# Expert rows added by TensorE in the second half of a gather, four routes moved to the first half, and copies moved to ScalarE

## The chip, the cores and the metric

The kernel runs on one core of a Trainium2 chip. The metric is the device time of one execution in microseconds. The core's engines work side by side and each takes its instructions in the order of its program: TensorE (matmuls, in the profile PE), VectorE (DVE), ScalarE (ACT), GpSimd (POOL) and SyncE (SP, which issues loads and stores). They wait for one another by semaphores. Matmul results go to eight PSUM banks of 128 x 512 float32.

## What is computed

512 tokens of width 1024 pass two blocks. The first block is a convolution mixer and then a layer of experts: each token has 8 heads, each head picks 16 of 16384 experts, and each expert is a row of u (1024 numbers) and a row of v (1024 numbers):

```
idx, gates = peer_route(q, sub_keys)          # 8 heads x 16 experts for every token
act = gelu(einsum("chkd,cd->chk", u[idx], xc))
out = einsum("chk,chkd->cd", act * gates, v[idx])
```

The second block is a feed-forward layer (hidden 2816), two causal attentions side by side (a forget-gate one, and a latent one with rotary parts), a gated mix, an output product and another feed-forward layer, over the 512 tokens.

## The kernel before, in words

Tokens stand on the 128 partitions in four tiles (t = 0 to 3). The expert layer is a loop over 512 "rows". Row i is head and choice (16 rows to a head, 8 heads to a tile): one indirect DMA by GpSimd gathers, for the 128 tokens of the tile, u and v of one chosen expert each (1 MB) into one of 7 `pair` buffers. Groups of 16 rows are one route (head n of 32). For every row:

- `dot(i)` on VectorE (the custom instruction of line 1321) multiplies u with the token and sums;
- `weigh(i)` on ScalarE makes the weight in five small activations (all activations have line 1384);
- in the first half (rows 0 to 255, tiles 0 and 1) ScalarE makes a diagonal of the weights (`diag`), and TensorE adds weight times v into a pair of banks ("mix") by two matmuls of 512 columns, which the profile shows as four records; in the second half (rows 256 to 511, tiles 2 and 3) VectorE adds it to `resid` itself, two rows later (`add_row`, line 827);
- then the buffer is free and GpSimd issues the gather of row i+7 into it (line 1862).

`route(n)` on VectorE finds the 16 best experts of head n in 24 small steps. It runs during the 16 rows before, four steps a row for six rows; GpSimd can't gather row 16n before. Index and gate buffers are four deep.

Chain A is the whole second block for tiles 0 and 1 (256 tokens). It runs in the second half of the gather, chain B (tiles 2 and 3) behind the gather. Each engine has the chain's steps in the same order. `plan_banks()` writes by hand which PSUM bank each step uses and when it is due on a plan clock in us: feed-forward 1 from 0 to 244, norm before the projections from 252, projections to 327, the 32 looks (a look is query times key for one head and one tile of queries) from 330.2 to 429.4 every 3.2 us, gates, branches and output to 558, feed-forward 2 to 802. `clock(row)` turns a row's number into this clock, 3.3 us a row from row 268 on. VectorE, ScalarE and GpSimd go through rows and, behind each row, do all chain steps due by its clock (`Paced.until`). TensorE has no rows in the second half and goes through chain A as fast as data come.

A look's path in attention: TensorE look n, VectorE its row's least (line 1144), ScalarE the exponential, TensorE turns the result of look n-3, VectorE copies the turned one (line 1151), TensorE multiplies with the values (n-4). During the first 16 looks `prepared` also makes the latent heads out of two banks, four steps a look, on all engines.

Weights come in 1 MB chunks through three buffers, issued by SyncE, a chunk when the one three before it has been used.

The lines that matter:

```
                for k in range(16):
                    i = 16 * n + k
                    dot(i)
                    if i >= HALF + 2:
                        add_row(i - 2)
                    for _ in range(4):
                        next(steps, None)
                    ...
                    first.until(clock(i))
```

Of the kernel before, what the change touches and what calls it, by code (L numbers as in the profile page):

```python
# [7 lines left out]
P = 128  # L8
# [77 lines left out]
ROW_US = 3.3  # L86
START_ROW = 268
# [11 lines left out]
class Plan:  # L99
# [14 lines left out]
    def ring(self, stage, n, us=0.0):  # L114
        self.add(stage, [(self.at + j) % 8 for j in range(n)], us)
        self.at = (self.at + n) % 8
# [6 lines left out]
def plan_banks():  # L123
    p = Plan()
    for stage, n in (("norm0", 10), ("cf", 16), ("sc", 16), ("bg", 4), ("ms_sc", 1), ("mean", 1), ("wout0", 4),
                     ("var", 1), ("ms_cf", 1), ("wout1", 4)):
        p.ring(stage, n)
    p.add("hn", [0, 1])
    for c, (h, a, b) in enumerate(CALLS):
        p.add("q", [0, 1])  # L130
        p.add("S", [2, 3])
        if c == 0:
            p.add("hn", [0, 1, 2, 3, 0, 1])
    for t in range(2):
        p.add("mix", [4, 5] if t % 2 == 0 else [6, 7], told=False)
    p.clock = 0.0
    for x in "AB":
        p.at = 0

        def ffn(f):  # L140
            p.clock += 8.0
            p.ring(f"norm{f}{x}", 4, 1.5)
            p.ring(f"up{f}{x}", 22, 7.0)
            p.ring(f"down{f}{x}", 4, 19.0)

        ffn(1)
        p.clock += 8.0
        for stage, n, us in (("norm_m", 4, 1.5), ("lat", 2, 5.0), ("fq", 2, 7.0), ("fv", 2, 7.0), ("cum", 1, 3.0),
                             ("tfq", 4, 1.0), ("fk", 2, 7.0), ("tfk", 4, 2.0), ("tlat", 2, 1.0)):
            p.ring(stage + x, n, us)  # L150
        p.add("look" + x, [0, 1] * 16, 3.2)
        p.add("turn" + x, [2, 3] * 16)
        p.add("prep" + x, [6, 7] * 8)
        for blk in range(4):
            p.add("o" + x, [4 + blk % 2], told=False)
            p.add("fin" + x, [4 + blk % 2], 4.0)
        p.at = 0
        for stage, n, us in (("gate", 8, 7.0), ("br", 16, 1.8), ("wo", 4, 7.0)):
            p.ring(stage + x, n, us)
        ffn(2)  # L160
    return p
# [62 lines left out]


def clock(row):

    return (row - START_ROW) * ROW_US


def program(nc, x, meta, wts, uv, rows, cols, pos, ident, tri, mask, out):
    with ExitStack() as ctx:
# [98 lines left out]
        MISC, CHAIN, PAIR = 2048, 3216, RAW - 2048 * NPAIR  # L331
# [19 lines left out]
        gat = ar("gat", MISC + 992, 64).rearrange("p (b n) -> p b n", b=4)  # L351
        idx = ar("idx", MISC + 1056, 64, U).rearrange("p (b n) -> p b n", b=4)
        sm = ar("sm", MISC + 1120, 16).rearrange("p (b n) -> p b n", b=4)
# [13 lines left out]
        fsq = ar("fsq", LAYER + 9728, 1024)  # L367
        fsg = [ar(f"fsg{i}", LAYER + 10752 + 256 * i, 256) for i in range(2)]
# [5 lines left out]
        YM = [ar(f"ym{i}", LAYER + 8704 + 512 * i, 512) for i in range(2)]  # L374
        PTB = {"A": [ar(f"pta{i}", LAYER + 9728 + 256 * i, 256) for i in range(4)],
# [48 lines left out]
        def taken(e, stage, n):  # L424

            b = B[stage, n]
            e.wait_ge(outs[b.bank], b.after)

# [45 lines left out]
        def products(e):  # L474
# [122 lines left out]
            scores(2)  # L597
            for i in range(HALF):
                t, r = divmod(i, 128)
                if i % 16 == 0 and i // 16 < 6:  # L600
                    scores(i // 16 + 3)
                e.wait_ge(diagd, i + 1)
                for h in range(2):
                    if r == 0:
                        fresh("mix", 2 * t + h)
                    b = B["mix", 2 * t + h]
                    ins = mm(bank[b.bank][:], diag[i % 8], pair[i % NPAIR][:, 1024 + h * 512:1536 + h * 512], r == 0,
                             r == 127)
                ins.then_inc(v_used, 1)
# [8 lines left out]
            def rows_times(stage, n0, pieces, lhs, ready=None, width=512):  # L618
# [3 lines left out]
                for key, nk in pieces:  # L622
                    w = piece(key, nk)
# [15 lines left out]
            def normed(k):  # L639
                for i in range(2):  # L640
                    turned_rows(k, "norm" + k if k[0] != "m" else "norm_" + k, i, frow[i])
# [5 lines left out]
            def ffn(f, p):  # L647
                normed(f"{f}{p}")
                turned_in(f"norm{f}{p}")
                for c in range(22):  # L650
                    w = piece((f"f{f}", c, p), 8)
# [6 lines left out]
                for h in range(2):  # L658
                    rows_times(f"down{f}{p}", 2 * h, [((f"d{f}", h * 6 + q, p), 4 if q < 5 else 2) for q in range(6)], H,
                               None if h else lambda kt: taken(e, f"up{f}{p}", kt))  # L660
# [8 lines left out]
            def chain(p):  # L669
                t0, nth = T0[p], NTH[p]  # L670
                ffn(1, p)
                normed("m" + p)
                turned_in("norm_m" + p)
                rows_times("lat" + p, 0, [(("lat", 0, p), 4), (("lat", 1, p), 4)], FT, width=360)
                rows_times("fq" + p, 0, [(("fqkv", 0, p), 4), (("fqkv", 1, p), 4)], FT)
                rows_times("fv" + p, 0, [(("fqkv", 4, p), 4), (("fqkv", 5, p), 4)], FT)
# [6 lines left out]
                ins.then_inc(done, 1)  # L683
                e.wait_ge(ext_q, 4 * (nth + 1))
                for i in range(2):
                    heads_turned("tfq" + p, 2 * i, 66, FQ[:, i])
                rows_times("fk" + p, 0, [(("fqkv", 2, p), 4), (("fqkv", 3, p), 4)], FT)
                e.wait_ge(ext_k, 4 * (nth + 1))
                for i in range(2):
                    heads_turned("tfk" + p, 2 * i, 66, FQ[:, i])  # L690
                e.wait_ge(lat_scaled, 2 * (nth + 1))
                for i in range(2):
                    o, done = fresh("tlat" + p, i)
# [3 lines left out]
                attention(p)  # L697
                for c in range(8):
                    w = piece(("gate", c, p), 8)
# [6 lines left out]
                for c in range(4):  # L706
                    yt = YFT if c % 2 else YMT
                    if c == 0:
                        for blk in range(4):
                            taken(e, "fin" + p, blk)  # L710
                    w = piece(("br", c, p), 4)
                    for j in range(4):
                        o, done = fresh("br" + p, 4 * c + j)
# [3 lines left out]
                for h in range(2):  # L717
                    rows_times("wo" + p, 2 * h, [(("wo", 2 * h, p), 4), (("wo", 2 * h + 1, p), 4)], MT,
                               None if h else lambda kt: e.wait_ge(m_add, 8 * nth + kt + 1))
                ffn(2, p)  # L720


# [27 lines left out]
            def attention(p):  # L750
                t0, nth = T0[p], NTH[p]
                prep = prepared(p)
                for i in range(2):
# [5 lines left out]
                for n in range(38):  # L759
                    if n == 16:  # L760
# [47 lines left out]

            chain("A")
            chain("B")  # L810


        def vector(e):
# [319 lines left out]
            def attention(p):  # L1133
                t0, nth = T0[p], NTH[p]
                prep = prepared(p)
                for n in range(38):
# [8 lines left out]
                    if 3 <= n < 35:  # L1145
# [114 lines left out]
            def used(i):  # L1260

                if i <= HALF:
                    e.wait_ge(v_used, i)
                else:
                    e.wait_ge(added, i - HALF)

            def route(n):

                t_, h, r = n // 8, n % 8, n % 4
# [15 lines left out]
                if n >= 4:  # L1285
                    used(16 * (n - 3))
# [37 lines left out]
            def add_row(i):  # L1324
# [3 lines left out]
                if i > HALF:  # L1328
                    e.wait_ge(added, i - HALF)
                stt(r, pair[i % NPAIR][:, 1024:2048], wgt[:, i % 8:i % 8 + 1], r, ALU.mult, ALU.add).then_inc(added, 1)  # L1330

            def mixed_in(t):

                e.wait_ge(v_used, 128 * (t + 1))
# [17 lines left out]
            for n in range(32):  # L1352
                steps = route(n + 1) if n < 31 else iter(())
                for k in range(16):
                    i = 16 * n + k
                    dot(i)
                    if i >= HALF + 2:
# [3 lines left out]
                    if n and n % 8 == 0:  # L1361
                        if k == 2 and n <= 16:
                            mixed_in(n // 8 - 1)
                        if k == 6:
                            final_mean(n // 8 - 1)
                        if k == 9:
                            final_row(n // 8 - 1)
                    first.until(clock(i))
                for _ in steps:
                    pass  # L1370
            for i in (PAIRS - 2, PAIRS - 1):
                add_row(i)
            first.until(1e9)
            final_mean(NT - 1)
# [5 lines left out]
        def scalar(e):  # L1380
# [127 lines left out]
            def normed(k, p, ready):  # L1508
                stage = "norm" + k if k[0] != "m" else "norm_" + k
                t0 = T0[p]  # L1510
                for i in range(2):
                    yield when(stage, 0) - 9.0
                    ready(i)
                    squared(k, i, resid[:, t0 + i, :], fsq)
# [66 lines left out]
            def attention(p):  # L1581
                t0, nth = T0[p], NTH[p]
                prep = prepared(p)
                for n in range(38):
# [4 lines left out]
                    if n < 32:  # L1589
# [5 lines left out]
                        if h == 0 and n >= 16:  # L1595
# [3 lines left out]
                            accum_out=ls[a][:, h:h + 1]).then_inc(out_, 1)  # L1599
                    if n < 16:  # L1600
# [108 lines left out]
            def gates(n):  # L1709
                r = n % 4  # L1710
# [3 lines left out]
            def final_row(t):  # L1714
                if t < 2:
                    for h in range(2):
                        taken(e, "mix", 2 * t + h)
                else:
                    e.wait_ge(added, 128 * (t - 1))
                act(HN[t], resid[:, t, :], ACT.Square, accum_out=nss[:, FINAL + t:FINAL + t + 1]).then_inc(fin_sq, 1)  # L1720

            def weigh(i):
# [9 lines left out]
                act(h_, a, ACT.Copy, scale=gat[:, n % 4, k:k + 1]).then_inc(curved, 1)  # L1732
# [9 lines left out]
            for n in range(32):  # L1742
                if n < 6:
                    scores(n + 3)
                for k in range(16):
                    i, j = 16 * n + k, (16 * n + k) % 8
                    weigh(i)
                    if i < HALF:
                        if i >= 8:
                            e.wait_ge(v_used, i - 7)  # L1750
                        e.wait_ge(weighed, i + 1)
                        act(diag[j], idt[:], ACT.Copy, scale=wgt[:, j:j + 1]).then_inc(diagd, 1)
                    if k == 4 and n < 31:
                        gates(n + 1)
                    if k == 3 and n and n % 8 == 0:
# [8 lines left out]
        def pool(e):  # L1764
# [88 lines left out]
            for i in range(PAIRS):  # L1853
# [4 lines left out]
                if NPAIR <= i < HALF + NPAIR:  # L1858
                    e.wait_ge(v_used, i - NPAIR + 1)
                elif i >= HALF + NPAIR:  # L1860
                    e.wait_ge(added, i - NPAIR + 1 - HALF)
                e.indirect_dma_start(pair[i % NPAIR], None, uv, bass.IndirectOffsetOnAxis(  # L1862
                    ap=idx[:, n % 4, k:k + 1], axis=0)).then_inc(pairs_in[i % NPAIR], 16)
                if i > 128 and i % 128 == 12:
# [132 lines left out]
```

## Time and profile before

| | |
|---|---|
| median of 3 runs | 2866.18 us (2854.21 to 2866.60) |
| profiled execution | 2865.02 us |
| its span, first to last instruction | 2863.2 us |
| granted TensorE clock, mean (1 is 2.4 GHz) | 0.906 |
| TensorE matmuls busy | 2312.3 us (81%) |
| VectorE busy | 1629.2 us (57%) |
| ScalarE busy | 1009.8 us (35%) |
| DMA | 758.73 MB, mean 265 GB/s |

Busy time is summed over an engine's instructions; it says nothing about who waits. By VectorE's dots row 0 stands at 336 us, row 256 at 1067, row 344 at 1397, row 368 at 1501, row 398 at 1655 and row 511 at 2078.

### The profile page before, as it was taken

How to read it: one execution, taken by the hardware profiler on the slowest of the kernel's cores; microseconds unless marked ns; L12 is line 12 of the kernel's file. 1: busy time of each engine (PE TensorE's matmuls, PEld its weight loads, DVE VectorE, ACT ScalarE, POOL GpSimd, SP SyncE). 2: the span in 40 equal slices, each digit the busy share in tenths (PEclk: the TensorE clock that was granted, in tenths of full speed). 3: DMA queues.
4: the chain of work that ended last, by engine and by line, in shares of the span. 5: the costliest groups of instructions: out<-in, count | busy, mean ns of one | idle time of the engine just before them, and what ended most of it. 6: DMA issues, size and time to landing. Idle time of an engine off the chain costs nothing.

```text
span 2863.2 us, 25889 instructions
## 1 busy us (share of the span) xinstructions
PE 2312.3 (81%) x8344; PEld 1502.4 (52%) x8344; DVE 1629.2 (57%) x3312; ACT 1009.8 (35%) x3503; POOL 814.2 (28%) x623
## 2 busy tenths in 40 slices
PE   6756888887877773999354598699689997999999
PEld 6744533332222222884222376587278644786884
DVE  3994445546777769877887989887620013501000
ACT  4222255456666664433443443443310012310000
POOL 3651134345555553323342332322200001000000
PEclk9878999999999996999675589899889997799999
DMA  4210478879999998999874789999924431033443
GB/s 157 74 44 15 162 292 361 345 301 421 421 421 421 421 418 315 408 421 420 340 300 147 279 342 421 371 419 420 415 108 148 153 138 41 30 118 135 159 147 132
DMA packets 107159, 758.73 MB, mean 265 GB/s; under 512 B 12032, under 2 KB 12800, under 8 KB 16400
## 3 DMA queue, kind: packets, MB, share of 16 engines
q0 software_dynamic: 73728, 536.90, 46.5%
q1 hardware_dynamic: 33296, 220.18, 20.1%
q8 instruction: 66, 1.08, 0.1%
q14 instruction: 69, 0.57, 0.1%
HBM read 754.94 MB, written 2.10 MB: 264 GB/s over the span
## 4 chain that ended last, share of the span: by engine, by line
PE 42%; DVE 27%; DMA 18%; issue 6%; ACT 5%; POOL 1%; DVEq 0%; SPq 0%; ACTq 0%; POOLq 0%
PE bank L476 41%; DMA pair<-in_uv,idx 18%; DVE resid L827 6%; DVE pair L1321 6%; DVE acc L827 4%; ACT smalls L1384 1%; ACT diag L1384 1%; DVE qm L821 1%; DVE ohb L821 1%; POOL smalls L1825 1%; DVE idu L1248 1%; PE bank L666 0%; DVE scores L1251 0%; DVE idu L1257 0%; PE bank L496 0%
## 5 line engine op out<-in xcount | busy, mean ns | idle before, releaser
L1862 POOL DMA_INDIRECT pair<-in_uv,idx x512 | 636.7, 1244 | 994.9 <-DVE resid L827 586.3
L1384 ACT ACTIVATE smalls<-smalls 128x1 f32<-128x1 f32 x2056 | 540.8, 287 | 727.6 <-DVE smalls L1321 705.9
L1321 DVE CUSTOM_DVE_ANT_0 pair<-pair,hn 128x1024 f32<-128x1024 f32 x512 | 623.8, 1220 | 286.2 <-DMA pair<-in_uv,idx 281.6
L476 PE MATMUL bank<-ft,raw 128*128 128x256 f32 x3328 | 727.1, 382 | 15.2 <-DVE ft L821 15.2
L476 PEld LDWEIGHTS bank<-ft,raw 128*128 128x128 f32 x3328 | 637.3, 192 | 104.1 <-issue 16.3
L476 PE MATMUL bank<-pair,diag 128*128 128x512 f32 x1024 | 500.0, 622 | 126.9 <-ACT diag L1384 126.9
L476 PEld LDWEIGHTS bank<-pair,diag 128*128 128x128 f32 x1024 | 180.6, 192 | 442.5 <-ACT diag L1384 299.8
L827 DVE SCALAR_TENSOR_TENSOR resid<-pair,smalls,resid 128x1024 f32<-128x1024 f32 x256 | 327.5, 1279 | 0.2
L476 PE MATMUL bank<-raw,hidden 128*128 128x512 f32 x704 | 302.8, 592 | 0.0
L476 PEld LDWEIGHTS bank<-raw,hidden 128*128 128x128 f32 x704 | 133.8, 190 | 166.7 <-issue 166.5
L821 DVE TENSOR_TENSOR hidden<-fsg,bank 128x256 f32<-128x256 f32 x88 | 36.9, 420 | 318.5 <-ACT fsg L1384 317.3
L476 PE MATMUL bank<-xt,half 128*128 128x264 f32 (+1 forms) x864 | 126.1, 311 | 23.5 <-DVE zpad L821 21.0
L1777 POOL TENSOR_TENSOR smalls<-smalls,mh 128x1 f32<-128x1 f32 (+1 forms) x21 | 16.6, 794 | 449.3 <-DVE smalls L824 449.3
L1384 ACT ACTIVATE smalls<-smalls,gat 128x1 f32<-128x1 f32 x512 | 143.0, 279 | 0.0
L496 PE MATMUL bank<-idt,frow 128*128 128x128 f32 x96 | 21.6, 417 | 149.2 <-ACT frow L1384 149.2
L1384 ACT ACTIVATE fsg<-bank 128x256 f32<-128x256 f32 x88 | 33.1, 377 | 307.0 <-PE bank L476 307.0
L476 PEld LDWEIGHTS bank<-xt,half 128*128 128x128 f32 x864 | 120.2, 202 | 29.4 <-DVE zpad L821 17.8
L827 DVE SCALAR_TENSOR_TENSOR acc<-upad,colt,acc 128x512 f32<-128x512 f32 x90 | 123.0, 1367 | 3.0
L476 PE MATMUL bank<-ht,raw 128*128 128x512 f32 (+2 forms) x288 | 114.4, 559 | 1.4 <-ACT ht L1384 1.4
L476 PE MATMUL bank<-raw,ft 128*128 128x512 f32 (+1 forms) x256 | 104.9, 571 | 8.5 <-DVE ft L821 8.5
L1384 ACT ACTIVATE diag<-idt,smalls 128x128 f32<-128x128 f32 x256 | 102.8, 402 | 23.5 <-ACT smalls L1384 0.4
L1771 POOL TENSOR_TENSOR half<-raw,half 128x2048 fp32r<-128x2048 f32 x14 | 66.7, 4770 | 155.2 <-ACT half L1384 155.2
(208 smaller groups left out, 1986.9 us busy)
## 6 DMA issues: line engine op xcount, KB each, us to landing
raw<-in_wts SPq DMA_DIRECT2D x194, 1024.0 KB
pair<-in_uv,idx POOLq DMA_INDIRECT x512
raw<-in_wts SPq DMA_DIRECT2D x10, 512.0 KB
raw<-in_wts SPq DMA_DIRECT2D x4, 720.0 KB
resid<-in_x SPq DMA_DIRECT2D x4, 512.0 KB, 5.4
out<-resid SPq DMA_DIRECT2D x8, 256.0 KB
raw<-in_wts SPq DMA_DIRECT2D x2, 768.0 KB
rowt<-in_rows SPq DMA_DIRECT2D x1, 1204.0 KB, 13.1
```

Source lines behind the costliest of these rows:

```text
L476: return e.matmul(o, a, b, start=start, stop=stop)
L496: ins = e.transpose(o[:, j * P:j * P + n], src[0:n, kt * P:(kt + 1) * P], idt[0:n, 0:n])
L821: return e.tensor_tensor(o, a, b, op)
L827: return e.scalar_tensor_tensor(out=o, in0=a, scalar=s, in1=b, op0=op0, op1=op1)
L1248: e.max_index(di[:, 0:8], dst[:, 0:8], src).then_inc(v_step, vs_.up())
L1321: e.tensor_tensor_reduce(b[:, 0:1024], b[:, 0:1024], HN[i // 128], 1.0, 0.0, ALU.mult, ALU.add, actv[:, i % 8:i % 8 + 1]).then_inc(dotted, 1)
L1384: return e.activation(o, i, f, **kw)
L1771: e.tensor_tensor(half(s)[:, 1, 0:c.n], wbufs[c.slot][:, 0:c.n], half(s)[:, 0, 0:c.n].bitcast(F), ALU.subtract).then_inc(w_lo, 1)
L1777: e.tensor_tensor(nrs[0:n, c:c + 1], nqs[0:n, c:c + 1], mh[0:n, 0:1], ALU.pow).then_inc(n_rs, 1)
L1825: e.tensor_tensor(sm8[(3 * j + 2) % 12][:, 0:k], sm8[(3 * j + 1) % 12][:, 0:k], mh[:, 0:k], ALU.pow).then_inc(hn_rs, 1)
L1862: e.indirect_dma_start(pair[i % NPAIR], None, uv, bass.IndirectOffsetOnAxis(ap=idx[:, n % 4, k:k + 1], axis=0)).then_inc(pairs_in[i % NPAI ...
```

## The change

- `ON_PE` says for every row who adds its v. In the second half it is TensorE for rows 256 to 266 and 338 to 395 (69 rows), VectorE for the rest. `UP_TO[i]` counts how many rows before i each has added, and all waits for "row i is used" go by it.
- TensorE interleaves: it walks the second half's rows, adds those that are its own, and behind each row does the chain's steps due by `clock(i) + LEAD`, LEAD = 16; each chain step on TensorE has now a due time. Up products are due 7 us before VectorE's due, and so 23 us ahead on the clock; a step of the looks is due at VectorE's due less 1 plus LEAD, that is 1 us ahead.
- Tiles 1, 2 and 3 use banks 6 and 7 for their sums; chain A's ring has banks 0 to 5 instead of all eight, and its preparation of heads one bank (5) instead of two.
- Diagonals of the second half's rows use the tiles `onest` and `maskf` in turn; ScalarE waits until all but one earlier row of TensorE's are added.
- The rate is 3.36 us a row from row 262 on instead of 3.3 from row 268.
- Groups 9, 11, 13 and 15 do two routes each, at rows 0 and 8 of the group. Groups 27 to 31 have none. Index and gate buffers are eight deep.
- The turned copies of chain A's attention (line 1151) are activations of ScalarE.
- Squares of chain A and B norms are written to `frow` instead of a tile of their own; a tile's bank sums are added to `resid` behind dot 1 of the next tile (instead of 2), for tiles 2 and 3 too.

```diff
-ROW_US = 3.3
-START_ROW = 268
+ROW_US = 3.36
+START_ROW = 262
+LEAD = 16.0
+def clock(row):
+    return (row - START_ROW) * ROW_US
+ON_PE = [i < HALF or clock(i) < 14.0 or 255.0 < clock(i) < 450.0 for i in range(PAIRS)]
+TWICE = (9, 11, 13, 15)
+ROUTES = [[r for r in range(n + 1 + sum(b < n for b in TWICE), n + 2 + sum(b <= n for b in TWICE)) if r < 32]
+          for n in range(32)]
+UP_TO = [(sum(ON_PE[:i]), i - sum(ON_PE[:i])) for i in range(PAIRS + 1)]
...
+            def add_row(i):
+                t = i // 128
+                begun, done = UP_TO[128 * t][0] == UP_TO[i][0], UP_TO[i + 1][0] == UP_TO[128 * t + 128][0]
+                e.wait_ge(diagd, UP_TO[i + 1][0])
+                for h in range(2):
+                    if begun:
+                        fresh("mix", 2 * t + h)
+                    b = B["mix", 2 * t + h]
+                    ins = mm(bank[b.bank][:], diag_of(i), pair[i % NPAIR][:, 1024 + h * 512:1536 + h * 512], begun, done)
+                ins.then_inc(v_used, 1)
...
                 for n in range(38):
+                    yield when("look" + p, min(n, 31)) + LEAD - 1.0
...
-            chain("A")
-            chain("B")
+            first = Paced(chain("A"))
+            for i in range(HALF, PAIRS):
+                if ON_PE[i]:
+                    add_row(i)
+                first.until(clock(i) + LEAD)
+            first.until(1e9)
+            for _ in chain("B"):
+                pass
...
(VectorE)
-                    if 3 <= n < 35:
+                    if p == "B" and 3 <= n < 35:
...
-                    if i >= HALF + 2:
+                    if i >= 2 and not ON_PE[i - 2]:
                         add_row(i - 2)
...
(ScalarE)
+                    if p == "A" and 3 <= n < 35:
+                        r = n - 3
+                        w = (t0 + r % 16 // 8 + 1) * P
+                        if r >= 4:
+                            e.wait_ge(mixed, 32 * nth + r - 3)
+                        o, out_ = filled(e, "turn" + p, r)
+                        act(PTB[p][r % 4][:, 0:w], o[:, 0:w], ACT.Copy).then_inc(out_, 1)
...
-                    if i < HALF:
+                    if ON_PE[i]:
                         if i >= 8:
-                            e.wait_ge(v_used, i - 7)
+                            e.wait_ge(v_used, UP_TO[i][0] - (7 if i < HALF else 1))
                         e.wait_ge(weighed, i + 1)
-                        act(diag[j], idt[:], ACT.Copy, scale=wgt[:, j:j + 1]).then_inc(diagd, 1)
+                        act(diag_of(i), idt[:], ACT.Copy, scale=wgt[:, j:j + 1]).then_inc(diagd, 1)
```

## Rows read from the trace of the kernel before

**Rows 1.** The page's slices of 71.6 us: what DMA moved.

```profile
GB/s 157 74 44 15 162 292 361 345 301 421 421 421 421 421 418 315 408 421 420 340 300 147 279 342 421 371 419 420 415 108 148 153 138 41 30 118 135 159 147 132
```

**Rows 2.** Stretches: us, then busy us (instructions) by engine; clock, DMA share, GB/s.

```profile
1067.00:1364.00 297.00, 236.31 (x901) 173.07 (x900) 247.71 (x458) 116.39 (x450) 96.74 (x83) 0.90 0.97 392
1364.00:1666.00 302.00, 152.07 (x496) 94.59 (x496) 249.37 (x578) 123.53 (x470) 100.53 (x86) 0.62 0.72 268
1666.00:2090.00 424.00, 351.99 (x1354) 262.79 (x1355) 349.21 (x626) 167.40 (x636) 118.45 (x112) 0.91 0.95 389
2090.00:2863.00 773.00, 738.28 (x3000) 543.80 (x2998) 120.32 (x307) 86.34 (x206) 22.76 (x23) 0.95 0.33 121
...
1067.00:1117.00 50.00, 3.48 (x12) 2.02 (x12) 47.03 (x90) 23.76 (x91) 23.96 (x18) 0.58 0.85 323
...
1426.00:1501.00 75.00, 45.19 (x128) 23.18 (x126) 62.09 (x151) 31.06 (x113) 32.58 (x23) 0.80 0.81 306
```

**Rows 3.** VectorE's waits, 1067 to 1364, then 1666 to 2090: us, times, longest.

```profile
DVE pair L1321 <- DMA pair<-in_uv,idx: 30.6, 24, 2.5
...
DVE pair L1321 <- DMA pair<-in_uv,idx: 48.7, 40, 2.5
```

**Rows 4.** Stretches of group 15: rows 240 to 245, 246 to 255.

```profile
1026.66:1043.05 16.39, 11.95 (x25) 4.06 (x24) 15.73 (x49) 9.59 (x39) 8.50 (x7) 1.00 1.02 423
1043.05:1067.15 24.10, 19.41 (x40) 6.85 (x40) 12.24 (x21) 15.36 (x60) 13.54 (x10) 1.00 1.01 411
```

**Rows 5.** Timeline (start, us), one first-half row through VectorE, ScalarE, TensorE.

```profile
1031.73 1.22 DVE L1321 CUSTOM_DVE_ANT_0 pair<-pair,hn 128x1024 f32<-128x1024 f32 x1
...
1032.99 0.29 ACT L1384 ACTIVATE smalls<-smalls 128x1 f32<-128x1 f32 x2 [0.86 <-DVE smalls L1321]
...
1034.26 0.40 ACT L1384 ACTIVATE diag<-idt,smalls 128x128 f32<-128x128 f32 x1
...
1034.71 1.98 PE L476 MATMUL bank<-pair,diag 128*128 128x512 f32 x4 [0.55 <-ACT diag L1384]
```

**Rows 6.** Timeline of VectorE: tile 1's bank sums, then a row in the looks.

```profile
1076.13 1.27 DVE L821 TENSOR_TENSOR resid<-bank,resid 128x512 f32<-128x512 f32 x2
...
1606.12 0.27 DVE L1144 TENSOR_REDUCE smalls<-bank 128x1 f32<-128x128 f32 x1
1606.31 0.41 DVE L1151 COPY pta<-bank 128x256 f32<-128x256 f32 x1
...
1606.64 1.21 DVE L1321 CUSTOM_DVE_ANT_0 pair<-pair,hn 128x1024 f32<-128x1024 f32 x1
...
1607.78 1.28 DVE L827 SCALAR_TENSOR_TENSOR resid<-pair,smalls,resid 128x1024 f32<-128x1024 f32 x1
...
1608.98 0.08 DVE L1257 MATCH_VALUE_LOAD idu<-vals,scores 128x8 f32 x1
```

**Rows 7.** TensorE's groups, 1398 to 1501: busy, mean ns, idle before.

```profile
L476 PE MATMUL bank<-raw,ft 128*128 128x512 f32 x96 | 41.9, 596 | 0.0
L476 PE MATMUL bank<-raw,ft 128*128 128x360 f32 x32 | 11.7, 531 | 7.4 <-DVE ft L821 7.4
L666 PE MATMUL bank<-idt,fq 128*66 128x128 f32 x32 | 7.2, 419 | 29.8 <-DVE fq L1069 29.8
L496 PE MATMUL bank<-idt,frow 128*128 128x128 f32 x16 | 3.8, 428 | 40.3 <-ACT frow L1384 40.3
```

**Rows 8.** Timeline of TensorE: a head's product, a look with mask, a look.

```profile
1503.33 1.84 PE L476 MATMUL bank<-raw,qlt 128*128 128x384 f32 x4 [0.24 <-ACT klt L1384]
...
1587.55 0.65 PE L476 MATMUL bank<-kftA,qft 66*128 66x256 f32 x2
1588.04 0.22 PE L476 MATMUL bank<-maskb,idb 128*128 128x128 bf16 x1
...
1596.44 1.17 PE L476 MATMUL bank<-kftA,qft 66*128 66x256 f32 x2
```

**Rows 9.** Waits, 1602 to 1666.

```profile
PE bank L476 <- DVE pta L1151: 27.2, 16, 3.9
```

More of the change, by code:

```diff
@@ L112, in add, with ring @@
             self.uses[stage, n + j] = Use(b, self.outs[b] - 1, self.fills[b], self.outs[b], self.clock)
-    def ring(self, stage, n, us=0.0):
-        self.add(stage, [(self.at + j) % 8 for j in range(n)], us)
-        self.at = (self.at + n) % 8
+    def ring(self, stage, n, us=0.0, size=8):
+        self.add(stage, [(self.at + j) % size for j in range(n)], us)
+        self.at = (self.at + n) % size
 CALLS = [(0, 0, 1), (1, 0, NT), (0, 1, NT)] + [(h, 0, NT) for h in range(2, 8)]
@@ L133, in plan_banks @@
             p.add("hn", [0, 1, 2, 3, 0, 1])
-    for t in range(2):
-        p.add("mix", [4, 5] if t % 2 == 0 else [6, 7], told=False)
+    for t in range(NT):
+        p.add("mix", [6, 7] if t else [4, 5], told=False)
     p.clock = 0.0
     for x in "AB":
-        p.at = 0
+        p.at, size = 0, 6 if x == "A" else 8
         def ffn(f):
             p.clock += 8.0
-            p.ring(f"norm{f}{x}", 4, 1.5)
-            p.ring(f"up{f}{x}", 22, 7.0)
-            p.ring(f"down{f}{x}", 4, 19.0)
+            p.ring(f"norm{f}{x}", 4, 1.5, size)
+            p.ring(f"up{f}{x}", 22, 7.0, size)
+            p.ring(f"down{f}{x}", 4, 19.0, size)
         ffn(1)
@@ L149, in plan_banks @@
                              ("tfq", 4, 1.0), ("fk", 2, 7.0), ("tfk", 4, 2.0), ("tlat", 2, 1.0)):
-            p.ring(stage + x, n, us)
+            p.ring(stage + x, n, us, size)
         p.add("look" + x, [0, 1] * 16, 3.2)
         p.add("turn" + x, [2, 3] * 16)
[L153 to L156, printed above, removed]
+        if x == "A":
+            p.add("o" + x, [4] * 4, told=False)
+            p.add("prep" + x, [5] * 14)
+            p.add("fin" + x, [5], 4.0)
+            p.add("prep" + x, [5] * 2)
+            p.add("fin" + x, [5] * 3, 4.0)
+        else:
+            p.add("prep" + x, [6, 7] * 8)
+            for blk in range(4):
+                p.add("o" + x, [4 + blk % 2], told=False)
+                p.add("fin" + x, [4 + blk % 2], 4.0)
         p.at = 0
         for stage, n, us in (("gate", 8, 7.0), ("br", 16, 1.8), ("wo", 4, 7.0)):
-            p.ring(stage + x, n, us)
+            p.ring(stage + x, n, us, size)
         ffn(2)
@@ L647, in ffn @@
             def ffn(f, p):
-                normed(f"{f}{p}")
+                yield from normed(f"{f}{p}")
+                yield when(f"norm{f}{p}", 3) + LEAD
                 turned_in(f"norm{f}{p}")
                 for c in range(22):
+                    yield when(f"up{f}{p}", c) - 7.0
                     w = piece((f"f{f}", c, p), 8)
@@ L696, in chain @@
                     e.transpose(o[:, 2 * P:3 * P], LAT[:, i, 192:320], idt[:]).then_inc(done, 1)
-                attention(p)
+                yield from attention(p)
                 for c in range(8):
+                    yield when("gate" + p, c) - 7.0
                     w = piece(("gate", c, p), 8)
@@ L1714, in final_row @@
             def final_row(t):
[L1715 to L1719, printed above, removed]
+                for h in range(2):
+                    taken(e, "mix", 2 * t + h)
                 act(HN[t], resid[:, t, :], ACT.Square, accum_out=nss[:, FINAL + t:FINAL + t + 1]).then_inc(fin_sq, 1)
```

124 lines of the change are left out of this document (67 added, 57 removed).

## The prediction

> **What bounds the kernel now.** I read the page first, then the kernel cut into stretches, then the engines inside the worst stretch. In the page's slices [rows 1] the reader is to see three regimes: a gather that reaches 421 GB/s in slices 10 to 14, a part with a dip to 147 GB/s in the twenty-second, and from the thirtieth on the little traffic of weights alone. The stretches [rows 2] measure it. The gather's first half (to 1067 us) fills DMA. From 2090 on TensorE is busy 738 of 773 us; nothing of the change is in there. Between them lie the 256 rows of the second half, 1023 us: at 392, 268 and 389 GB/s. Against 421 GB/s these are short by 7%, 36% and 8%, which is 20, 110 and 32 us. So 162 us is all that relief of engines can give behind 1067 us, and two thirds of it lies in 1364 to 1666, where chain A makes its projections and its attention. There VectorE is busy 249 of 302 us and TensorE 152, at a granted clock of 0.62. In the two others the gather's own landing is what VectorE waits for (30.6 and 48.7 us) [rows 3]: there DMA is the limit.
>
> The change's window, rows 338 to 395, is that middle stretch: with the new clock, chain A's time 252 (norm before the projections) falls on row 337, 330 (first look) on row 360, 429 (last look) on row 390. In the old numbering they were rows 344, 368 and 398, with their dots at 1397, 1501 and 1655 us.
>
> **The change part by part.**
>
> *Four routes under the first half.* A row there takes 2.5 us. The window of six rows with a route is 16.39 us, DVE busy 15.73 [rows 4]; without 6 dots of 1.14 each (1606.64 to the next instruction at 1607.78, [rows 6]) a route costs 9.5 us. The ten rows behind it leave DVE busy only 12.24 of 24.10 us, so 11.9 idle. A second route of 9.5 just fits, with 2.4 left, and seven pair buffers carry a lag of a few us. Groups 9, 11, 13, 15 pay about 0.5 us each: +2 us, bounds 0 and +10 (all slack missed by 2.5 us in each). The four routes are gone from rows 432 to 495, where DMA is full for most of the time (48.7 us of DVE's waits are for it): their 38 us of DVE buy what the 32 us of missing DMA allow. I take -10, bounds -32 and 0.
>
> *Rows 256 to 266 on TensorE.* VectorE loses 11 adds of 1.20 (1607.78 to 1608.98, [rows 6]), 13 us; TensorE is idle here (3.5 of 50 us busy in 1067 to 1117, and DMA at 323 GB/s, [rows 2]). DMA's lack in that window is 50*(1-323/421) = 12 us. But row 256's matmul waits for a bank that DVE empties behind dot 257, and the diagonals go through two tiles. I take -6, bounds -12 and 0.
>
> *Rows 338 to 360: projections.* The chain's own TensorE work between 1398 and 1501 is 41.9+11.7+7.2 and 7.4 in six small groups, of which the first has 3.8, together 68 us, and its waits for VectorE in between are 7.4 and 29.8 us [rows 7]: 105 us in all. Each add costs TensorE 1.98 us [rows 5]; 23 of them are 46. They can fill 37 us of those waits, 9 stick out: the stretch is now TensorE's own 114 us. VectorE's relief of 23*1.20 = 28 us has nobody waiting for it then. I take +9; bounds -28 (the waits were DVE's and shrink with it) and +46 (no overlap).
>
> *Rows 361 to 390: the looks.* This decides. TensorE now takes chain A's steps at due times: look n behind the add of the first row whose clock is at least its due less 1 us; VectorE takes the row's least of look n behind the dot of the first row whose clock is at least its due. Looks are due 3.2 us apart from 330.2, rows 3.36 us apart from row 262. Working the 32 through, looks 0 to 5 and 21 to 26 stand one row ahead on TensorE; the other 20 (6 to 20, 27 to 31) stand behind the add of the very row after whose dot VectorE wants them. There a ring closes that did not exist: dot i, five activations, the diagonal, the add, the look, its reduction, and only then dot i+1, all in program order. Its length from rows: dot at 1031.73, first activation at 1032.99, diagonal at 1034.26 for 0.40, add at 1034.71 for 1.98, that is 4.96 us [rows 5]; the look with its mask 0.7 (1587.55 to 1588.26, [rows 8]); the reduction 0.2 until the next instruction (1606.12 to 1606.31, [rows 6]). Together 5.9 us a row. Before, a row without other chain work cost VectorE dot 1.14, add 1.20, reduction 0.2, turned copy 0.3 and a route's share of 0.6 (9.5/16): 3.4, and TensorE waited for VectorE there (27.2 us for the turned copies), not the reverse [rows 9]. So +2.5 for each of 20 looks: +50. Four of the eight steps that also prepare a latent head lie in the ring (the first at look 8); their product (1.84 us, [rows 8]), run ahead before, now comes behind the look: +7. The twelve others lose add and copy (1.5), of which I count 1.4 each: -17. Sum +40. Bounds: -45 if the ring never holds (all 32 lose 1.4), and +74 if TensorE is granted the lower clock throughout: a look of the same shape took 0.65 us at the upper level and 1.17 at the lower [rows 8], so the add would take 3.5 instead of 1.98 and the look some 0.3 more, 1.7 to 1.8 on 20 rings. The middle stretch ran at 0.62 with TensorE half idle; with adds it is busy about 3.6 of 5.9 us, and 1426 to 1501 with 45 busy of 75 us had 0.80 [rows 2], so I stay near the upper level.
>
> *Turned copies on ScalarE* are counted above (32 of 0.33 us, 1606.31 to 1606.64, [rows 6]); ScalarE is busy 124 of 302 us [rows 2], and the copy falls between the exponential and the next row's activations. *Heads' preparation in one bank* makes TensorE and ScalarE alternate; it stands behind waits already there. *Six banks instead of eight for chain A's ring* lets TensorE run 6 fills ahead: DMA limits those stages. Squares into frow, deeper index buffers, shifted addresses: nothing, no other user is then alive.
>
> *Rows 391 to 395* put 10 us of adds on a TensorE that is busy 352 of 424 us from there on [rows 2]; they need not be on the path, and take 6 from VectorE: +3, bounds -6 and +10. *The end*: one more bank pair is added behind row 511, 1.27 us for both halves [rows 6]: +1.
>
> *Sum:* 2-10-6+9+40+3+1 = +39. The profiled execution took 2865.0 us around its span of 2863.2, 1.2 below the median of 2866.2, so 2904 us.
>
> The Trainium skill ("Perfetto Trace Analysis", section "Identifying the Most-Contended Engine") says to take the engine with the highest occupancy as the bottleneck and optimize it first; by that rule, VectorE with 249 of 302 us is it, and the change would win its whole relief, as in rival 1. That the stretch before was VectorE's agrees with the trace. The rule says nothing of a ring that the relief itself ties.
>
> **The rivals.**
> 1. *The relief arrives (faster).* If look n is in its bank by the time VectorE has done dot and route of its row, the ring is slack, and 58 adds of 1.20 and 32 copies of 0.33 come off the path in the middle stretch: -80, with -6, -10 and +6 (2+3+1) as above 2865-90 = 2775; at most 110 us are there. It decides from the point where the ring of 5.9 is shorter than VectorE's and DMA's row, 2.5 to 3.4 us, or where TensorE stands a row ahead for most looks. For it: VectorE 83% busy, TensorE half idle. Against it: the order of the instructions.
> 2. *They cancel.* The ring holds only where no route or preparation is in the row (then VectorE has own work in it): 10 rings instead of 20 give -25, and the projections -9: 2870.
> 3. *TensorE drops to the lower clock in the looks:* +34: 2938, and with the projections' adds slowed (9 of 23 sticking out, 1.4 each, and their own products) 2960.
> 4. *The pacing goes wrong elsewhere*, for instance TensorE's next weights start later, since its steps are paced now: +20 to +60 in the last stretch. Also slower.
>
> **How the numbers follow.** Forecast 0.50 (own range 2875 to 2940), rival 1 0.23, rival 2 0.13, rivals 3 and 4 together 0.14. Slower by over 0.5% (about what a measurement of this kernel tells from no change, 14 us): 0.45 of the forecast's, all of 3 and 4, 0.01 of 2: 0.60. Within: 0.05 and 0.09: 0.14. Faster: 0.23 and 0.03: 0.26. A range from 2805 to 2955 leaves out rival 1's deeper half (0.13) and the far end of 3 and 4 (0.06).
>
> **What would show it.** Right: in the looks, DVE waits for PE (look banks) that sum to over 40 us, rows 366 to 380 and 386 to 390 at 6 us or more, rows 361 to 365 and 381 to 385 at 3 to 4; the pair issues on POOL wait for PE; DMA in the middle stretch no higher than before; first-half groups still 2.5 us a row. Wrong: a middle stretch of 220 to 240 us at over 330 GB/s, with no DVE wait for a look; or a ring that is closed but short, which would mean the activations or the add start earlier than in rows 5.

## The result, and the profile after

The changed kernel takes 2945.73 us (median of 4 runs, 2941.12 to 2950.16) where the kernel before took 2865.76: ratio 1.0289, interval 1.0257 to 1.0320. It is 80 us slower; the prediction had 2904, 39 slower. Its profiled execution has a span of 2945.8 us. Behind row 511's dot every kernel here does the same chain B, yet that part takes 774 to 780 us in seven of the thirteen traces and 785 to 788 us in the other six, with the granted clock at 0.76 to 0.80 and at 0.69 to 0.71 from 300 to 400 us behind that dot, so small steps are also given from row 256 to row 511, where this doesn't enter.

The page's slices (73.6 us each), what DMA moved; they answer to [rows 1]. The dip is no longer one slice of 147 but four of 121 to 217:

```profile
GB/s 152 72 43 29 157 331 361 313 370 421 421 421 421 416 377 408 421 420 342 279 121 171 172 217 420 383 421 420 421 170 155 140 147 68 29 100 137 149 157 128
```

Both kernels cut at the same points of chain A's plan clock, so that a stretch holds the same steps of the chain: row 256 to clock 0, 0 to 252 (feed-forward 1), 252 to 330 (projections), 330 to 430 (looks), then to row 511. First the kernel before (us; busy of PE, PEld, DVE, ACT, POOL with counts; granted clock; DMA share; GB/s):

```profile
1067.00:1105.00 38.00, 2.14 (x5) 0.68 (x4) 37.20 (x76) 15.63 (x66) 16.31 (x12) 0.60 0.86 333
1105.00:1398.00 293.00, 234.33 (x897) 172.55 (x898) 240.76 (x451) 113.56 (x432) 88.62 (x80) 0.90 0.97 393
1398.00:1501.00 103.00, 65.82 (x188) 35.75 (x188) 82.42 (x181) 43.44 (x158) 44.98 (x32) 0.78 0.83 314
1501.00:1656.00 155.00, 78.46 (x279) 52.43 (x278) 129.97 (x319) 63.87 (x252) 45.47 (x44) 0.56 0.61 220
1656.00:2078.00 422.00, 358.32 (x1380) 267.73 (x1379) 348.65 (x630) 164.26 (x637) 118.69 (x111) 0.91 0.97 398
```

and the changed one, which answers to [rows 2]:

```profile
1064.00:1083.00 19.00, 13.38 (x30) 5.09 (x29) 18.38 (x54) 11.26 (x42) 8.56 (x8) 1.00 0.99 390
1083.00:1357.00 274.00, 241.22 (x919) 173.06 (x917) 220.82 (x407) 112.82 (x428) 84.51 (x76) 0.95 0.99 408
1357.00:1472.00 115.00, 99.70 (x258) 48.19 (x258) 65.09 (x189) 50.69 (x172) 39.06 (x33) 0.92 0.74 280
1472.00:1711.00 239.00, 144.96 (x417) 76.02 (x415) 90.54 (x266) 82.38 (x315) 46.09 (x45) 0.74 0.42 153
1711.00:2158.00 447.00, 365.46 (x1403) 268.09 (x1403) 323.41 (x492) 167.11 (x674) 129.83 (x117) 0.92 0.95 390
```

The looks carry the loss: 239 us instead of 155, with VectorE's work down from 130 to 91 us and more idle than busy. The projections take 12 more. The two stretches ahead take 293 instead of 331, mostly since they hold 7 rows fewer by the new clock; the last one has those rows back and takes 25 more. What VectorE waited for in the looks (us in total, times, longest), before, where VectorE's waits hold none for a look (here its two longest):

```profile
DVE smalls L1034 <- ACT tmp L1384: 8.0, 7, 3.7
DVE pair L1321 <- PE bank L476: 4.2, 1, 4.2
```

and after, with GpSimd's wait to issue gathers:

```profile
DVE smalls L1204 <- PE bank L506: 109.9, 26, 7.6
POOL pair L1924 <- PE bank L506: 77.9, 17, 8.4
```

Line 1204 is the reduction of a look. One turn of the ring, row 375, in the timeline (start, us). Of the lines left out, only ScalarE's other small activations are on the ring:

```profile
1616.01 1.22 DVE L1380 CUSTOM_DVE_ANT_0 pair<-pair,hn 128x1024 f32<-128x1024 f32 x1
...
1617.27 0.30 ACT L1443 ACTIVATE smalls<-smalls 128x1 f32<-128x1 f32 x2 [0.30 <-DVE smalls L1380]
...
1618.54 0.40 ACT L1443 ACTIVATE onest<-idt,smalls 128x128 f32<-128x128 f32 x1
...
1619.00 3.78 PE L506 MATMUL bank<-pair,onest 128*128 128x512 f32 x4 [2.74 <-ACT onest L1443]
...
1622.57 1.06 PE L506 MATMUL bank<-kftA,qft 66*128 66x256 f32 x2
...
1623.42 0.31 PE L506 MATMUL bank<-maskb,idb 128*128 128x128 bf16 x1
...
1623.78 0.42 DVE L1204 TENSOR_REDUCE smalls<-bank 128x1 f32<-128x256 f32 x1 [6.54 <-PE bank L506]
...
1624.12 1.22 DVE L1380 CUSTOM_DVE_ANT_0 pair<-pair,hn 128x1024 f32<-128x1024 f32 x1
```

From dot to dot 8.1 us: 2.99 to the add, as in [rows 5]; 3.57 from there to the look, where a first-half row's add lasts 1.98; 1.16 for look and mask instead of 0.7; 0.4 until the next dot, for the reduction. Rows 375 to 380 take 7.3 to 8.5 us each. The granted clock was 0.74 over the stretch, and five of these six adds lasted 3.5 to 3.8 us, at the lower of the two levels (1.2 GHz). The turn before, row 374, had its add at the upper level, and it took 5.84 us from dot (1610.17) to dot (1616.01):

```profile
1613.16 1.98 PE L506 MATMUL bank<-pair,maskf 128*128 128x512 f32 x4 [2.85 <-ACT maskf L1443]
1614.98 0.60 PE L506 MATMUL bank<-kftA,qft 66*128 66x256 f32 x2
```

### The profile page after: what moved, and what is told of

It is laid out like the page before. It is cut to its first block, busy times and chain, and to the rows that moved or that the text cites. A ratio compares the mean times of both kernels' runs of the same rounds, so it can differ in the third digit from the quotient of the medians.

```text
span 2945.8 us, 26453 instructions
## 1 busy us (share of the span) xinstructions
PE 2429.4 (82%) x8620; PEld 1538.7 (52%) x8620; DVE 1543.2 (52%) x3215; ACT 1033.8 (35%) x3598; POOL 795.2 (27%) x623
## 4 chain that ended last, share of the span: by engine, by line
PE 48%; DVE 20%; DMA 19%; ACT 7%; issue 5%; POOL 1%; DVEq 0%; ACTq 0%; SPq 0%; POOLq 0%
PE bank L506 47%; DMA pair<-in_uv,idx 19%; DVE pair L1380 5%; DVE acc L887 4%; DVE resid L887 3%; ACT smalls L1443 3%; ACT diag L1443 1%; DVE qm L881 1%; POOL smalls L1889 1%; PE bank L526 1%; PE bank L707 0%; DVE ohb L881 0%; DVE smalls L1204 0%; PE bank L839 0%; DVE ysc L887 0%
## 5 line engine op out<-in xcount | busy, mean ns | idle before, releaser
L1924 POOL DMA_INDIRECT pair<-in_uv,idx x512 | 616.4, 1204 | 1025.3 <-PE bank L506 542.0
L506 PE MATMUL bank<-pair,diag 128*128 128x512 f32 x1024 | 494.0, 616 | 129.1 <-ACT diag L1443 128.9
L887 DVE SCALAR_TENSOR_TENSOR resid<-pair,smalls,resid 128x1024 f32<-128x1024 f32 x187 | 239.4, 1280 | 5.1 <-ACT smalls L1443 4.9
L506 PE MATMUL bank<-pair,maskf 128*128 128x512 f32 x136 | 85.3, 760 | 49.1 <-ACT maskf L1443 45.6
L506 PE MATMUL bank<-pair,onest 128*128 128x512 f32 x140 | 85.6, 743 | 46.0 <-ACT onest L1443 43.3
L1204 DVE TENSOR_REDUCE smalls<-bank 128x1 f32<-128x128 f32 (+3 forms) x64 | 31.2, 490 | 149.8 <-PE bank L506 149.8
```

Source lines behind the costliest of these rows:

```text
L506: return e.matmul(o, a, b, start=start, stop=stop)
L887: return e.scalar_tensor_tensor(out=o, in0=a, scalar=s, in1=b, op0=op0, op1=op1)
L1204: e.tensor_reduce(mx[a][:, h:h + 1], o[:, 0:(t + 1) * P], X, ALU.min).then_inc(least, 1)
```

## The experiments

Each ran beside the kernel before on the same chip; different experiments ran on different chips, where the kernel before took 2861.3 to 2865.8 us. Ratios are to the kernel before, with a 95% interval. A stretch is measured between VectorE's dots at the same plan clocks as above, with the clock read between rows, so that the looks are 238.2 us in the changed kernel and 154.6 before.

**Looks one row ahead.** The due times of TensorE's looks, 3.4 us earlier:

```diff
-                    yield when("look" + p, min(n, 31)) + LEAD - 1.0
+                    yield when("look" + p, min(n, 31)) + LEAD - 4.4
```

(and the same in the step that opens the stretch.)

> TensorE's steps of the looks are due 3.4 us earlier (due less 4.4 instead of less 1), so that each of the 32 looks stands before the add of its own row; all 69 rows stay on TensorE. Theory (a ring of about 7.9 us through dot, activations, add at the lower clock, look and reduction): VectorE's waits for looks fall from 88.7 us to under 30, the stretch of the looks from 238 us to about 175, the time to 2880. Rival (the load of the adds on TensorE at the lower clock costs, in whatever order): under 20 us less, 2925 to 2945. Rival (one bank for the heads' preparation): no change, 2945.

Measured 2873.55 us, ratio 1.0043 (1.0023 to 1.0062). The looks take 165.6 us instead of 238.2, and VectorE's waits for them over the stretch, 35.5 us instead of 109.9:

```profile
DVE smalls L1204 <- PE bank L506: 35.5, 16, 9.3
```

The work is the same, all 69 rows stay on TensorE, only the order differs, and 72 of the 80 us are gone. The ring is the cause of them: the load of the adds and the one bank are the same in both kernels. The gain also lies in the rows where the prediction put the rings: rows 366 to 380 take 91.0 us instead of 145.2 and rows 386 to 390 24.4 instead of 42.0, the ten other rows (361 to 365, 381 to 385) 57.2 instead of 62.2. The stretch's windows line shows a higher clock with the same work, and TensorE busy 73% of the time instead of 61%:

```profile
1475.00:1640.00 165.00, 120.38 (x413) 64.85 (x414) 88.14 (x262) 80.49 (x312) 46.57 (x44) 0.84 0.56 208
```

**12 rings instead of 20.** `LEAD - 2.2` in the same two places.

> The same steps due 1.2 us earlier (due less 2.2): 12 looks instead of 20 stand behind the add of their own row (6 to 12, 27 to 31). Ring theory: eight rings of 7.9 us become rows of 4 to 5, 26 us less, 2920. Load or one bank: 2945.

Measured 2917.84 us, 1.0205 (1.0156 to 1.0253); looks 212.8 us. With 20, 12 and 0 rings the looks take 238, 213 and 166 us: 3.2 us for each of the first eight rings undone and 3.9 for each of the twelve others. By rows it is the freed ones that gain: rows 373 to 380 take 28.3 us instead of 61.4, while rows 366 to 372 take 87.2 (83.8 in the changed kernel) and 386 to 390 42.1 (42.0).

**No adds of TensorE in the looks.** `ON_PE` with `255 < clock < 329 or 432 < clock < 450` in place of `255 < clock < 450`.

> Rows 360 to 390 go back to VectorE; 256 to 266, 338 to 359 and 391 to 395 stay on TensorE. Ring theory: without adds there is no ring; the looks take 155 to 165 us again instead of 238, 2945 - 80 = 2865. Rival (the paced looks, the one bank or the copies on ScalarE cost, not the adds): VectorE's 31 adds come on top of it, 2945 or more.

Measured 2873.71 us, 1.0058 (1.0036 to 1.0080); looks 168.8 us. So adds and order together are needed for the loss; but with the order mended the adds on TensorE win 3 us of the looks at most (165.6 against 168.8), where 31*1.20 = 37 us of VectorE's work had left. The 14 us over the kernel before that are left here (168.8 against 154.6) are taken up with the banks below.

**No adds of TensorE among the projections.** `329 < clock < 450`.

> Rows 338 to 359 go back to VectorE; 256 to 266 and 360 to 395 stay on TensorE. If the adds among the projections cost what the two traces differ there (115 us for the plan clock's 252 to 330 instead of 104), the time is 2935. If they relieve VectorE by 1.2 us each, 26 us more than now, 2970. The ring stays.

Measured 2933.22 us, 1.0252 (1.0203 to 1.0300). The projections take 100.7 us instead of 115.4; TensorE is busy for 65 of them and waits for the rest, and VectorE, with 22 adds more, is through the stretch 15 us sooner:

```profile
1360.00:1461.00 101.00, 65.13 (x182) 35.13 (x182) 89.89 (x213) 44.77 (x158) 40.92 (x33) 0.80 0.85 327
```

**Both.** Looks one row ahead and no adds among the projections.

> Looks one row ahead (due less 4.4) and, besides, no adds of TensorE among the projections (rows 338 to 359 back to VectorE). The two effects are in different stretches, so they should sum: 2873.5 less the 15 to 17 us that the projections' stretch lost when its adds went (115.4 to 100.7), 2857, about the kernel before. Rival (a look's stretch that starts earlier only waits longer for the weights or the gather): 2870 or more.

Measured 2854.08 us, 0.9970 (0.9956 to 0.9985). The two effects sum: from row 256 to row 511 the looks' order won 72.9 us (1094.6 to 1021.7) and the projections' adds 21.9 more (to 999.8).

**Half an add in the ring.** In rows 360 to 390 TensorE leaves out one of the two matmuls of v:

```diff
                 for h in range(2):
+                    if h == 0 and 360 <= i <= 390 and not begun and not done:
+                        continue
```

> Order as in the changed kernel (20 looks in the ring), but in rows 360 to 390 TensorE adds only the second 512 columns of v; the other half is left out. Ring theory: the add is one link of the ring and stands in it with its own length, 3.4 to 3.8 us at the lower clock; half of it takes 1.7 off each of 20 rings and 0.9 to 1.7 off rows bound by TensorE, 35 to 50 us less, 2900 to 2910. Rival (the wait for the diagonal and the semaphores is what costs): under 10 us less.

Measured 2932.65 us, 1.0248 (1.0220 to 1.0276), 13 less than the changed kernel and not 35 to 50. A turn at the lower level has lost what the theory says, row 374 here with 6.4 us from dot to dot where row 375 of the changed kernel took 8.1, with an add of 2.07 instead of 3.78. TensorE's line and VectorE's two:

```profile
1617.83 2.07 PE L506 MATMUL bank<-pair,maskf 128*128 128x512 f32 x2 [2.40 <-ACT maskf L1445]
```

```profile
1614.84 1.22 DVE L1382 CUSTOM_DVE_ANT_0 pair<-pair,hn 128x1024 f32<-128x1024 f32 x1
...
1621.24 1.22 DVE L1382 CUSTOM_DVE_ANT_0 pair<-pair,hn 128x1024 f32<-128x1024 f32 x1
```

But TensorE, with less to do, had a granted clock of 0.60 over the stretch instead of 0.74, and row 374 itself, which had run at the upper level in 5.8 us, took 6.4. The looks took 223 us instead of 238, and the rows with a ring (366 to 380 and 386 to 390) 170.4 instead of 187.2.

```profile
1483.00:1706.00 223.00, 131.92 (x355) 73.92 (x355) 89.72 (x264) 82.36 (x314) 45.62 (x45) 0.60 0.45 163
```

So the add is a link of the ring. My number for the whole took the clock as given; how much of the missing 20 to 35 us is the clock's was not measured apart.

**All adds back on VectorE.** `ON_PE = [i < HALF ...]`, the sums of tiles 2 and 3 in banks left out; the rest of the change stays. And the same with the heads prepared in two banks, free now, as before the change:

```diff
-            p.add("prep" + x, [5] * 14)
-            p.add("fin" + x, [5], 4.0)
-            p.add("prep" + x, [5] * 2)
-            p.add("fin" + x, [5] * 3, 4.0)
+            p.add("prep" + x, [6, 7] * 8)
+            p.add("fin" + x, [5] * 4, 4.0)
```

> All 256 rows of the second half are VectorE's, everything else as in the changed kernel (paced TensorE, ring of six, heads prepared in one bank, copies on ScalarE, four routes moved). Projections 101 us, looks 155 to 169, first rows 5 us more: 2860 to 2870. If the pacing or the ring of six cost by themselves, 2880 or more.

> As the one before, with the heads prepared in banks 6 and 7 as in the kernel before. The looks took 168.8 us without adds in them, 154.6 before. If the one bank is the cause: 10 to 14 us less than the one before, about 2852. If the copies on ScalarE or the due times are: no change.

Measured 2850.37 us (0.9968, 0.9953 to 0.9984) and 2834.57 us (0.9906, 0.9885 to 0.9928). The looks take 164.8 us with one bank and 152.2 with two. TensorE's timeline shows why: with one bank the second head product, the second turn and the second product of the other half wait for the first's bank to be emptied, and what stands behind them waits too,

```profile
1480.99 3.22 PE L506 MATMUL bank<-raw,qlt 128*128 128x384 f32 x4 [3.02 <-DVE qm L881]
...
1499.95 1.09 PE L707 MATMUL bank<-idt,qm 128*96 128x128 f32 x4 [3.76 <-ACT qmt L1442]
...
1506.86 2.07 PE L506 MATMUL bank<-raw,klt 128*128 128x512 f32 x2 [3.06 <-DVE qm L881]
```

while with two the first and second go through in one piece (4 and 2 records more in the last two groups, no wait between):

```profile
1475.71 3.17 PE L504 MATMUL bank<-raw,qlt 128*128 128x384 f32 x4
...
1493.08 1.91 PE L705 MATMUL bank<-idt,qm 128*96 128x128 f32 x8
...
1497.89 3.47 PE L504 MATMUL bank<-raw,klt 128*128 128x512 f32 x4 [2.90 <-ACT qmt L1440]
```

The first is 10 us below what was expected of it, so nothing shows that the pacing or the ring of six cost. The second takes 991.7 us from row 256 to row 511 where the first takes 1005.3, so the one bank costs 13.6 us there. The second kernel is the fastest of all: it beats the kernel before by 0.9%, and the changed one by 111 us, with none of the change's 69 rows on TensorE.

**What of the rest makes it faster.** Three single edits taken back from that kernel: the four routes (`TWICE = ()`), the copies on VectorE again, and the old rate (3.3 us a row from row 268).

> The kernel with all second-half adds on VectorE and heads prepared in two banks (2834.6 us), with one route in every group again. If the four routes of 9.5 us in rows 432 to 495 lay on VectorE's path: up to 38 us more, 2872. If the gather bounds there: 0 to 10 more, 2835 to 2845 (the prediction had 10 less the 2 of the first half).

Measured 2841.43 us (0.9933, 0.9911 to 0.9955), 7 more. All four times lie above the four of 2834.6's kernel, but those ran on another chip and the intervals of the ratios overlap. In the trace most of it is from clock 446 to row 511 (426 instead of 420 us), and the first half is the same.

> As that kernel, with the turned copies on VectorE again: 32 copies of 0.33 us on the engine that leads in the looks, 8 to 11 us more, 2843 to 2846; no change or less if ScalarE's later activations were the price of moving them.

Measured 2838.18 us (0.9917, 0.9890 to 0.9943), 4 more and not 8 to 11. The intervals overlap, so the medians don't tell it: its five times go from 2833.0 to 2853.2 us. The trace is of the longest, and 13.7 us of what it is longer lie behind row 511 (787.9 instead of 774.2), where the copies have no part. The looks take 155.2 us in it instead of 152.2.

> As that kernel, with the old rate of 3.3 us a row from row 268: chain A starts six rows later and ends with row 511 instead of 501. If the earlier start is what makes the 256 rows shorter (the stretch up to clock 252 took 15 us less than in the kernel before), 10 to 20 us more, 2845 to 2855; if DMA's bytes alone decide, no change.

Measured 2848.97 us (0.9962, 0.9946 to 0.9977), 14 more: of the 27 us by which the best kernel beat the one before on the same chip (2861.87), the new clock is the largest part. The edit has both the start and the rate in it, and they were not tried apart. From row 256 to row 511 it costs 11.3 us (1003.0 instead of 991.7), and 8.1 of these are in rows 501 to 510, 34.5 us instead of 26.4: with the new clock chain A's steps are all done by row 501, with the old one only behind row 511.

## Why the prediction was right and wrong

The side, the stretch and the mechanism were right; the time lies inside the range, but the forecast had less than half of the loss (39 of 80 us). The step that failed is the term of the looks: +40 was forecast and +84 measured. By the prediction's own steps:

- *Four routes:* +2 and -10 were forecast. The first half did not pay (a group with two routes took 40.5 us, VectorE busy 36.3 of them, still 419 GB/s); taking them back costs 7. Right within 2 us.

```profile
1023.30:1063.80 40.50, 29.96 (x62) 10.57 (x63) 36.28 (x107) 24.71 (x99) 18.63 (x16) 1.00 1.01 419
```

- *Rows 256 to 266:* -6 forecast. With these adds the stretch to clock 252 takes 293 us, without them (both kernels above) 301. Measured there it is -8, right; what became of it stands in the paragraph on the relief below.
- *Projections:* +9 forecast, +12 between the two traces, 15 when the adds are taken out alone, and 20 in the whole time when they are taken out of the kernel with looks ahead. The reason held, that TensorE's waits were too small for the adds and that nobody needed VectorE's relief. It is a little larger because the adds don't only fill waits: they also stand between the projections, and what ScalarE and VectorE make of these comes later. In the changed kernel VectorE waits 13.1 us for the latent rows and 19.1 for the squares that ScalarE makes for the heads' norms (3.1 and 1.1 without these adds):

```profile
DVE smalls L1094 <- ACT tmp L1443: 19.1, 4, 13.8
DVE smalls L881 <- ACT lat L1443: 13.1, 1, 13.1
```

- *The looks:* +40 forecast, +84 measured. This step failed in size, in three terms. (1) The ring: 20 times 2.5 us forecast, 72.6 us measured by opening it, 3.6 each. At the upper level the turn is the forecast's, 5.84 us in row 374 for 5.9. Most turns ran at the lower one: row 375 took 8.1, and 2.0 of the 2.2 more are TensorE's (1.6 in the add, 0.4 to 0.5 in look and mask). The prediction had this as a bound (+34) and put it aside with an argument from a stretch, 1426 to 1501 in the trace before, in which TensorE was busy in pieces of 22.5 and 14.3 us. In the ring it waits 1.9 to 3.7 us in every one of the turns of rows 374 to 380. (2) "Heads' preparation in one bank ... stands behind waits already there": it costs 12.6 us of the looks and 15.8 in all. The prediction did not follow the second product to its bank; it had counted only the first one's lateness (+7). (3) The 17 us won where no ring holds: 31 adds are worth 3 to 4 us of the looks at most (168.8 to 165.6, and 164.8 to 161.1 without adds among the projections), and the copies 3. From the kernel before to the changed one: 154.6, less 2.4 (copies, routes, clock and the rest together, to 152.2), plus 12.6 for the bank, 0.8 for all 69 adds with the looks ahead (to 165.6) and 72.6 for the ring are 238.2.
- *Ring of six: nothing; the new clock: no term.* The new clock is worth 14 us of gain. I had read only its effect on which rows meet which step, not that the chain now ends ten rows sooner, and that these rows then take 2.6 us each instead of 3.5.
- *The end:* +1 forecast; from row 511's dot to the end 787.4 instead of 785.3 us, a difference that can't be told from what executions differ by there.

Of the signs that the prediction named, VectorE's waits for looks (109.9 us, over 40 was said), GpSimd's waits for TensorE and the traffic in the looks (153 GB/s) came. Rows 366 to 380 and 386 to 390 took over 6 us in all but one (5.8), rows 381 to 385 3.5 on average. Rows 361 to 365 did not take 3 to 4 but 44.7 us together, among them row 361 with 17; with the looks ahead, too, they took 43.2, and in both kernels the heads' preparation begins in them.

So the runs give the steps below. The last three are each against 2834.6; from "no other adds" on the looks have the due times of the change again, where no add can close a ring:

| | median, us | step | row 256 to 511 in the trace | step |
|---|---|---|---|---|
| changed kernel | 2945.7 | | 1094.6 | |
| ring undone | 2873.6 | -72.2 | 1021.7 | -72.9 |
| no adds among the projections | 2854.1 | -19.5 | 999.8 | -21.9 |
| no other adds | 2850.4 | -3.7 | 1005.3 | +5.5 |
| two banks for the heads | 2834.6 | -15.8 | 991.7 | -13.6 |
| old clock back | 2849.0 | +14.4 | 1003.0 | +11.3 |
| routes back | 2841.4 | +6.9 | 999.4 | +7.7 |
| copies back | 2838.2 | +3.6 | 994.3 | +2.6 |

If the last three sum, they give 2859.5 us, 2 to 6 us from the kernel before (2861.9 and 2865.8 in two sets of runs), and 1013.3 for the trace, where the kernel before has 1010.7. What is left of the change (the ring of six, due times on TensorE, squares in `frow`) was not tried alone.

*What became of the relief.* With the looks ahead and none among the projections, TensorE adds 47 rows, 56 us of VectorE's work (2854.1); with no such add the time is 2850.4. By the traces 5.5 of the 56 us arrive at row 511, and behind it that kernel's trace took 786.6 us against 774.8, so the median doesn't tell them. Earlier in the trace more had been won: clock 446 is reached 19 us sooner (566.3 instead of 584.9 us after row 256), but from there to row 511 it takes 433.5 instead of 420.4 us. At that point VectorE goes through rows 391 to 395 in 1.15 us each, out of full buffers, and the next rows take 5.4, 8.6 and 7.3, with waits for the gather of 4.2 and 7.4; to row 511 it waits 84.3 us for the gather instead of 71.7. So a stretch that is cut at VectorE's dots can be up to seven rows, the number of buffers, ahead of what DMA has done.

In the looks the work moved and the pace stayed. Rows 373 to 380, behind the heads' preparation, take 25.8 us each way: first without adds on TensorE, where VectorE is busy 24.0 of them, then with adds and looks ahead, where TensorE is busy 23.6. DMA's share is 0.94 and 0.96, so the gather is near its limit there as well.

```profile
1573.29:1599.04 25.75, 18.88 (x83) 16.03 (x81) 24.02 (x44) 16.07 (x64) 11.46 (x9) 0.50 0.94 344
1584.06:1609.86 25.80, 23.57 (x113) 14.81 (x112) 14.79 (x36) 17.99 (x70) 11.68 (x11) 1.00 0.96 374
```

In rows 361 to 372, with the preparation, VectorE was busy only 61 of 100 us without the adds, so relief of it could win little: these rows took 108 us with the adds and 103 with none among the projections. The rule of the busiest engine, that the prediction set against its own (the Trainium skill, "Perfetto Trace Analysis", section "Identifying the Most-Contended Engine"), misled here: VectorE, with 130 of 155 us busy in the looks before, was relieved of 37 us of adds there, and the looks became 4 us shorter at best.

## What to carry to other kernels

When work moves to another in-order engine, write down for one round what stands behind it there and who waits for that: a relief that puts a link of the row loop ahead of something the relieved engine wants in the same row ties a ring, and the ring's length, not anyone's busy time, is then the pace. The cure was order: one row's lead. Price the links of such a ring at the clock that an engine gets which idles in each round. And if a change takes a buffer from another stage (here one of two banks), price that stage with its second item waiting for the first. Before counting relief as gain, look whether the engine that takes the work then needs as long for the row as the relieved one did, and whether the transfers have moved on by the end of the stretch.

## What the runs showed of the hardware

- The stretch with less to do had the lower clock: with half the matmuls of an add left out, the granted clock in the looks was 0.60 instead of 0.74, and 15 of a forecast 35 to 50 us were won; with the looks ahead and the same work it was 0.84, and with no adds 0.50. TensorE was busy 59%, 61%, 73% and 53% of these stretches. The Trainium skill ("Perfetto Trace Analysis", section "Matmul Optimizations") says that power follows utilization and that matmuls should run back to back; the four stretches agree.
- The same four records of an add took 1.98 us at the upper level and 3.78 at the lower (rows 374 and 375 of the changed kernel).
